# A space of 404 bytes between the one-hots of first and of second keys in the PEER layers

## What is computed

```python
def peer_ffn(hn, wq, subkeys, down, up):          # 8 heads, 128 keys a half, 16 of each kept
    q = (xt @ wq).reshape(N, H, 2, PEER_DKEY // 2)
    s = jnp.einsum('nhpd,hpkd->nhpk', q, subkeys)
    s_half, i_half = lax.top_k(s, K)
    ...                                           # the 16 best pairs (first key, second key), softmax: gate
    u = down[ec]
    act = gelu(jnp.einsum('cd,chkd->chk', xc, u)) * gc
    return jnp.einsum('chk,chkd->cd', act, up[ec])
```

## Time and profile before

| what | value |
|---|---|
| median of three runs | 2473.65 us |
| the profiled execution | 2462.88 us |
| its span | 2461.1 us |
| PE, DVE, ACT, POOL busy | 95%, 67%, 55%, 31% of the span |
| PE's share of the chain that ended last | 82% |
| HBM read | 380.79 MB, 155 GB/s over the span |

### The profile page before, as it was taken

One profiled execution on the slowest core, in us unless ns is written; L12 is line 12 of the kernel. 1 busy time (PEld: TensorE's weight loads), 2 busy tenths in 40 slices (PEclk: granted clock), 3 DMA queues, 4 the chain that ended last, 5 costly groups with the idle time before them and its releaser, 6 DMA issues.

```text
span 2461.1 us, 39024 instructions
## 1 busy us (share of the span) xinstructions
PE 2326.2 (95%) x15356; PEld 2105.1 (86%) x15356; DVE 1640.5 (67%) x3150; ACT 1343.0 (55%) x2505; POOL 759.4 (31%) x388
## 2 busy tenths in 40 slices
PE   6878989999999999999988978999999999999999
PEld 5776889999999888887957876799999999888887
DVE  4564557977788556666557475666967788566565
ACT  3344445468888554455543454244458888554544
POOL 3000002887777000000700053101887777000000
PEclk8888999999999999999999998999999999999999
DMA  5322234665555566665432343254665555666665
GB/s 176 125 81 83 89 108 152 192 183 165 166 165 166 194 189 193 191 191 168 153 113 92 123 138 112 69 169 149 189 188 163 164 164 164 195 189 194 190 191 159
DMA packets 109004, 384.39 MB, mean 156 GB/s; under 512 B 13055, under 2 KB 15920, under 8 KB 108376
## 3 DMA queue, kind: packets, MB, share of 16 engines
q1 hardware_dynamic: 108824, 381.91, 49.5%
HBM read 380.79 MB, written 1.06 MB: 155 GB/s over the span
## 4 chain that ended last, share of the span: by engine, by line
PE 82%; DVE 11%; ACT 4%; issue 1%; DMA 1%; POOL 1%; SPq 0%; DVEq 0%; ACTq 0%; POOLq 0%
PE psum L370 23%; PE psum L372 23%; PE psum L371 23%; PE psum L2042 2%; PE psum L402 2%; DVE weight_parts L343 1%; ACT weight_parts L338 1%; PE psum L2749 1%; PE psum L2969 1%; POOL weight_parts L349 1%; PE psum L616 1%; PE psum L1029 1%; PE psum L1468 1%; DVE hg_tmp L1075 1%; PE psum L1369 0%
## 5 line engine op out<-in xcount | busy, mean ns | idle before, releaser
L370 PE MATMUL psum<-acts_high,weight_parts 128*128 128x256 f32 x2872 | 821.0, 286 | 23.4 <-DVE weight_parts L343 10.8
L349 POOL TENSOR_TENSOR weight_parts<-weight_ring,weight_parts 128x1024 fp32r<-128x1024 f32 x276 | 670.2, 2439 | 483.6 <-ACT weight_parts L338 482.9
L372 PE MATMUL psum<-acts_high,weight_parts 128*128 128x256 f32 x2872 | 808.5, 282 | 0.0
L371 PE MATMUL psum<-acts_low,weight_parts 128*128 128x256 f32 x2872 | 808.5, 282 | 0.0
L338 ACT ACTIVATE weight_parts<-weight_ring 128x1024 fp32r<-128x1024 f32 x674 | 710.7, 1055 | 122.4 <-PE psum L372 59.2
L343 DVE TENSOR_TENSOR weight_parts<-weight_ring,weight_parts 128x1024 fp32r<-128x1024 f32 x398 | 489.2, 1230 | 297.0 <-ACT weight_parts L338 297.0
L370 PEld LDWEIGHTS psum<-acts_high,weight_parts 128*128 128x128 f32 x2872 | 551.7, 192 | 35.5 <-issue 12.1
L371 PEld LDWEIGHTS psum<-acts_low,weight_parts 128*128 128x128 f32 x2872 | 547.2, 191 | 1.4 <-issue 0.5
L372 PEld LDWEIGHTS psum<-acts_high,weight_parts 128*128 128x128 f32 x2872 | 546.5, 190 | 0.0
L372 PE MATMUL psum<-weight_parts,peer_coef 128*128 128x512 f32 x1024 | 403.5, 394 | 0.0
L371 PE MATMUL psum<-weight_parts,peer_coef 128*128 128x512 f32 x1024 | 401.4, 392 | 0.0
(11 more groups left out here) (428 smaller groups left out, 3005.7 us busy)
## 6 DMA issues: line engine op xcount, KB each, us to landing
weight_ring<-in_peer_down SPq DMA_DIRECT2D x128, 512.0 KB, 3.6
weight_ring<-in_peer_up SPq DMA_DIRECT2D x128, 512.0 KB, 3.5
weight_ring<-in_peer_u SPq DMA_DIRECT2D x128, 512.0 KB, 3.6
weight_ring<-in_peer_v SPq DMA_DIRECT2D x128, 512.0 KB, 3.7
weight_ring<-in_w_in SPq DMA_DIRECT2D x88, 512.0 KB, 3.6
weight_ring<-in_w_out SPq DMA_DIRECT2D x16, 512.0 KB, 3.6
weight_ring<-in_peer_w_q SPq DMA_DIRECT2D x16, 512.0 KB, 3.7
weight_ring<-in_w_in_v SPq DMA_DIRECT2D x10, 512.0 KB, 3.6
```

What stands on the lines that cost most here:

```text
L349: q.e.tensor_tensor(self.low, self.ring, self.high.bitcast(F32), ALU.subtract).then_inc(*self.unit.ready.once())
L370: q.e.matmul(out, sh, mh, start=first, stop=False)
L371: q.e.matmul(out, sh, ml, start=False, stop=False)
L372: return q.e.matmul(out, sl, mh, start=False, stop=last)
```

## The change

A tile of 404 bytes of each partition is opened between `first_keys` and `second_keys`. Nothing reads or writes it.

```diff
         with ExitStack() as inner:
             x.first = c.sb(name + "_first_keys", [P, 2, GROUP, P], inner, F32R)
+            c.sb(name + "_space_1", [P, 404 // 4], inner)
             x.second = c.sb(name + "_second_keys", [P, 2, GROUP, 2, P], inner, F32R)
```

## The result

The changed kernel takes 2457.75 us, the median of six runs (2453.2 to 2463.39); the kernel before takes 2473.44 beside it. The ratio is 0.994, with a 95% interval of 0.9925 to 0.9955: 15.7 us quicker by the medians, where 20 were forecast. The profiled execution took 2454.14 us.

The account below looks back on a forecast made before the run. PE was taken as the bound, by the distance between matmul starts. Terms summed to minus 20 us: 2442.9 against the profiled 2462.88, plus 10.8 for the median of runs, forecast 2453.6 us; range 2445 to 2475.

Parts of the forecast that it names:

- What bounds the kernel: PE, busy 95% of the span; one matmul stream in two rhythms, 113.3 or about 118 ns between starts.
- The place where the rhythm is lost: First four L2042 matmuls of each `peer`, at 542.95 and 1840.14 us; 2200 steps follow without return, 259.68 us each.
- if a group no longer breaks the quick rhythm: Condition of the gain in the one-hot stages: 2200 steps at 113.33 ns, 249.33 us instead of 259.68 per `peer`.
- term (2): Gain in both `peer` stages: twice 10.35 us, less 0 to 0.86 each for way in and out; 20 us taken.
- The mark named for it: Sign of being right: L2042 starts 0.45 us before the next L370 instead of 0.48; stage 249 to 251 us.
- always 120: Claim that matmuls at loaded minus streamed 0 modulo 512 always take 120 ns a step.
- Term (3): ACT, DVE, POOL and weight transfers follow a PE needing 249.3 us per stage; 88, 84, 77% busy, none ends last.
- one of the prediction's own signs of a wrong cause: In the one-hot stages, a shorter stream meets waits for ACT or POOL that were not there before.
- Term (4): Writers of second keys, L2014 and L2023, cost 0 at the new start; bounds 4 and 36 ns each.
- Rival A: Groups go on breaking the rhythm in the one-hot stages; at best 0.8 us saved, 2472.8 to 2473.7; chance 0.33.
- B: Some groups break the rhythm, others restore it; half the steps quick, minus 10 us, 2463.6; chance 0.10.
- C: Slower: the one-hot stream settles at 120 ns a step, plus 8.6 us, 2482.3; chance 0.07.

Follow-up runs that it names:

- alternating kernel: Kernel before, key buffers placed separately: first stage even groups 0, 0, 64, odd 0, 96, 160; second even 0, 0, 64, odd all 64; stages 254.64 and 259.26 us.
- last version: Changed kernel's distances (0, 96, 160) for even groups, 64 in all pairs for odd ones, up passes at 256; 2446.85 us, ratio 0.9903 against the kernel before.
- (0, 64, 128): Loaded minus streamed modulo 512 into, within and out of a group, set by 512 and 448 bytes of space in the first PEER layer; stage 259.25 us.
- (64, 160, 160): Loaded minus streamed modulo 512 into, within and out of a group, set by 64 and 352 bytes of space in the second layer; stage 252.92 us.
- all at 64: Spaces of 64 bytes before first keys and 448 between the keys, so every pair lies 64 apart modulo 512; 2460.99 us, ratio 0.9959 against the kernel before.

## Why the prediction was right, and where it was not

- **What bounds the kernel**, two rhythms of one stream, read from starts and not from durations: right. The counts moved from 426 to 440 in 50 us, and of the profiled executions only the two stages became shorter; the up passes kept 351.8 and 351.4 us.
- **The place where the rhythm is lost**, the first group, with the distance between loaded and streamed tile: right for the kernel before, and now tested. 512 bytes more, which leave all distances, leave the stage at 259.68 us, and spaces that change them decide the rhythm. Whether it is the distance or the place of a tile modulo 512 was not separated.
- **The step that failed: "if a group no longer breaks the quick rhythm"**, with 96 as a neighbour of the harmless 64. A group of the changed kernel disturbs PE and ends in the quick rhythm, whichever it found; that is shown by the alternating kernel and by the last version's first stage, which came in slow. Nearness to 64 is not what does it: (0, 64, 128) is slow, (64, 160, 160) quick, and all at 64 keeps what it finds. The forecast came out on the right side by another mechanism than the one it rested on, and that part was luck.
- **The size of term (2)**, 20 instead of 14.3 us: a group was priced at 0 to 13 ns (way in and way out), and takes 27 more than quick steps. Over 128 groups that is 3.5 us. The mark named for it, 0.45 us from L2042 to L370, did not come: it stayed at 0.48, and the stage took 252.5 us, not 249 to 251. The way in at 0 costs nothing of its own, as read from the earlier trace rows: 113 ns. So a distance of 0 is not "always 120", as the prediction had it.
- **Term (3), "nothing of this ends last"**: wrong near the end of the stage. Means over 260 us hid that DVE's work grows (38.50 us of 50 early in the stage, 43.01 late); 2.7 us in the two stages. By the times above PE does meet ACT and POOL there, and a shorter stream that meets such waits was one of the prediction's own signs of a wrong cause. It is one in part: it counts against this term, not against the two rhythms.
- **Term (4)**, the writers: right as far as seen. L2014 takes 681 ns in the median, as before, and L2023 369 instead of 368.
- **The Trainium skill's rule** (SBUF — State Buffer, "Who interferes with whom"), that PE's two read ports do not contend with anyone: the runs disagree as far as starts go. Tiles at other addresses, with no other difference, give stages of 252.5 or 259.7 us and up passes of 348 to 358.6 us. They do not show where in PE or the memory the time goes.
- Rival A was the nearest in one point: a blow in the group does come, in every group. That the same group then brings the quick rhythm back was in none of the cases. B, where some groups break it and others restore it, describes the alternating kernel, not the change; C did not come.
- The whole range, 2445 to 2475, holds A as well as the forecast, so that the time fell into it says little. The forecast's own range, 2445 to 2458, was just reached.

## What to carry to other kernels

Where matmuls run back to back, read the step from one start to the next and look for two values in one stream; 4.5 ns in 113, lost at one small foreign group of matmuls and not regained for 2200 steps, cost some 20 us here, of which the change got 14 back. A space between tiles, which costs no instruction, can decide it, but try several and look at the starts: the good distance of one stream (64 here) was among the worst of another. And when the steps of the bound engine get 4% shorter, check the others' work near the end of the stage, not as a mean over it.

## What the runs showed of the hardware

- One stream of 256-column matmuls ran at 113.3 or at 117.8 ns a step at a granted clock of 1.00 in every stretch shown, with the same tiles and places, and kept a rhythm until a wait or a foreign group; with groups at 64 in between, the slow one lasted 2319 steps, from a wait to the end of the stage.
- In groups with loaded minus streamed at 0 modulo 512 a step was 120 ns; but a way in at 0 took 113 ns out of the quick rhythm, and a way out at 0, after an inner 448, took 115. In one kernel PE changed rhythm 64 times in a stage, at every group.
- 512-column steps took 226.7 (0, 256), 229 (192, 448), 232.4 (128) and 233.3 ns (64, 320, 480) depending on that distance, or on where `coef` starts modulo 512; the pairs that lie 256 apart came out alike (64 and 320, 0 and 256, 192 and 448), which was not expected and was not followed up.
